# MLP products of a hybrid decoder layer: the first walks its moving operand and PSUM backwards, and the weights of both lie at other distances

## The reference

```python
h2 = rms_norm(x, pre_mlp_norm_w[layer])
a = jax.nn.relu(jnp.einsum("bsd,df->bsf", h2, w_ff1[layer]))
m_out = jnp.einsum("bsf,fd->bsd", a * a, w_ff2[layer])
x = x + rms_norm(m_out, post_mlp_norm_w[layer])
```

## Time and profile before

| | us |
|---|---|
| median of 2 runs | 2103.55 |
| lowest and highest | 2103.19, 2103.91 |
| the profiled execution | 2102.39 |
| its span, first to last instruction | 2100.2 |
| PE busy | 2070.8 |
| DVE busy | 1440.5 |
| ACT busy | 914.0 |
| POOL busy | 413.6 |

### The profile page before, as it was taken

One profiled execution on the slowest core, in us unless ns is written; L12 is line 12 of the kernel. 1 busy time (PEld: TensorE's weight loads), 2 busy tenths in 40 slices (PEclk: granted clock), 3 DMA queues, 4 the chain that ended last, 5 costly groups with the idle time before them and its releaser, 6 DMA issues. The chain is left out here.

```text
span 2100.2 us, 26863 instructions
## 1 busy us (share of the span) xinstructions
PE 2070.8 (99%) x10031; PEld 1736.0 (83%) x10031; DVE 1440.5 (69%) x1993; ACT 914.0 (44%) x1557; POOL 413.6 (20%) x252
## 2 busy tenths in 40 slices
PE   9999999999999999899999999999999999999998
PEld 9897878879788888688888788888888888888887
DVE  6897999889467777876667866666654536624285
ACT  6632434343444445745545644554431313313163
POOL 0000000000002312333332322332253034400012
PEclk9999999999999999999999999999999999999999
DMA  5121212113556875854455655445766455443376
GB/s 203 32 86 53 63 41 86 46 48 110 181 182 199 256 234 162 270 182 150 135 157 186 230 166 165 138 139 176 263 229 240 169 200 193 169 168 132 140 252 219
DMA packets 254143, 338.54 MB, mean 161 GB/s; under 512 B 11584, under 2 KB 195648, under 8 KB 240192
## 3 DMA queue, kind: packets, MB, share of 16 engines
q1 hardware_dynamic: 221376, 315.80, 45.1%
q10 hardware_dynamic: 32384, 20.98, 3.2%
q0 software_dynamic: 256, 0.07, 0.0%
HBM read 225.58 MB, written 111.21 MB: 160 GB/s over the span
## 5 line engine op out<-in xcount | busy, mean ns | idle before, releaser
L1953 PE MATMUL psum<-x_hi,w_hi_P 128*128 128x512 f32 x896 | 350.9, 392 | 10.7 <-DVE x_lo L1897 6.5
L1953 PE MATMUL psum<-x_lo,w_hi_P 128*128 128x512 f32 x896 | 349.8, 390 | 0.0
L2171 PE MATMUL psum<-w_hi,hid_hi 128*128 128x512 f32 x896 | 348.8, 389 | 0.9 <-DVE hid_lo L2049 0.9
L1953 PE MATMUL psum<-x_hi,w_lo_P 128*128 128x512 f32 x896 | 349.7, 390 | 0.0
L2171 PE MATMUL psum<-w_hi,hid_lo 128*128 128x512 f32 x896 | 348.6, 389 | 0.0
L2171 PE MATMUL psum<-w_lo,hid_hi 128*128 128x512 f32 x896 | 348.5, 389 | 0.0
L2049 DVE TENSOR_TENSOR hid_lo<-hid_raw,hid_hi 128x1024 fp32r<-128x1024 f32 x112 | 174.0, 1590 | 209.0 <-ACT hid_hi L2044 209.0
L2044 ACT ACTIVATE hid_hi<-hid_raw 128x1024 fp32r<-128x1024 f32 x112 | 113.0, 1051 | 342.5 <-DMA hid_raw<-scratch_hid 342.5
L1866 POOL TENSOR_TENSOR w_raw<-w_raw 128x512 f32<-128x512 f32 x128 | 181.2, 1440 | 409.3 <-DVE w_lo_P L1879 389.6
L1879 DVE TENSOR_TENSOR w_lo_P<-w_raw,w_hi_P 128x512 fp32r<-128x512 f32 x224 | 183.8, 833 | 106.5 <-ACT w_hi_P L1875 103.5
L1875 ACT ACTIVATE w_hi_P<-w_raw 128x512 fp32r<-128x512 f32 x224 | 136.8, 627 | 254.4 <-PE psum L1953 252.0
(11 more groups left out here) (284 smaller groups left out, 3814.7 us busy)
## 6 DMA issues: line engine op xcount, KB each, us to landing
scratch_hid<-stage SPq DMA_DIRECT2D x224, 256.0 KB, 3.7
hid_raw<-scratch_hid SPq DMA_DIRECT2D x56, 1024.0 KB, 4.9
w_raw<-in_w SPq DMA_DIRECT2D x52, 1024.0 KB, 5.0
w_grain<-in_w SPq DMA_DIRECT2D x48, 512.0 KB, 5.1
x_raw<-scratch_h2s SPq DMA_DIRECT2D x14, 1024.0 KB, 8.1
w_raw<-in_w_in SPq DMA_DIRECT2D x22, 512.0 KB, 3.6
scratch_h2s<-h2s SPq DMA_DIRECT2D x8, 1280.0 KB, 9.2
scratch_qk<-qout ACTq DMA_DIRECT2D x16, 512.0 KB, 3.4
```

Of the source, the lines that this page charges most:

```text
L1953: mm = nc.tensor.matmul(psum[:, bank_1(op, g), :], l, r, start=kt == 0 and i == 0, stop=kt == 3 and i == 2)
L2171: mm = nc.tensor.matmul(psum[:, bank, :], l, r, start=f == 0 and k == 0, stop=f == NFP - 1 and k == 2)
```

## The change

In the first product (`product`), the moving operand and the columns of PSUM are both indexed with `::-1`: the last token is read and written first, and each result lands at the address at which it landed before. The weight tiles move to other addresses, 128 bytes down and up again by 32 bytes after each third tile, so that there are five distances: w1_hi lies at -128, -96 and -64, w1_lo at -64, -32 and 0 bytes.

In the second product the slots of hid move: slot 0 by 256 bytes and another 16, slot 1 by 8, slot 2 by 0, and hid_lo and hid_raw of each slot by 32 more. The helper `hid_slot` allocates a tile with up to four floats more and leaves the first ones out. `acc` moves by 64 bytes, to make room.

```diff
-    w1_hi = {op: at(f"w1_hi_{op}", 69 + 2 * i, (4, P), F32R) for i, op in enumerate(OPS)}
-    w1_lo = {op: at(f"w1_lo_{op}", 83 + 2 * i, (4, P), F32R) for i, op in enumerate(OPS)}
+    w1_hi = {op: at(f"w1_hi_{op}", 68.875 + 2 * i + i // 3 / 32, (4, P), F32R) for i, op in enumerate(OPS)}
+    w1_lo = {op: at(f"w1_lo_{op}", 82.875 + 2 * i + (7 + i) // 3 / 32, (4, P), F32R) for i, op in enumerate(OPS)}
...
-    hid_at = [121, 48, 105]
-    hid_hi = [at(f"hid_hi{i}", kb, (NFP, P), F32R) for i, kb in enumerate(hid_at)]
-    hid_lo = [at(f"hid_lo{i}", kb + 8, (NFP, P), F32R) for i, kb in enumerate(hid_at)]
-    hid_raw = [at(f"hid_raw{i}", kb + 8, (NFP, P)) for i, kb in enumerate(hid_at)]
-    acc = [at(f"acc{t}", 64 + 4 * t if t < 10 else 97.5 + 4 * t, (D,)) for t in range(S // P)]
+    hid_at = [121 + 1 / 4, 48, 105]
+    hid_skip = [4, 2, 0]
+
+    def hid_slot(name, i, kb, dt=F32):
+        a = at(f"{name}{i}", kb, (NFP * P + hid_skip[i],), dt)
+        return a[:, hid_skip[i]:].rearrange("p (f t) -> p f t", f=NFP)
+
+    hid_hi = [hid_slot("hid_hi", i, kb, F32R) for i, kb in enumerate(hid_at)]
+    hid_lo = [hid_slot("hid_lo", i, kb + 8 + 1 / 32, F32R) for i, kb in enumerate(hid_at)]
+    hid_raw = [hid_slot("hid_raw", i, kb + 8 + 1 / 32) for i, kb in enumerate(hid_at)]
+    acc = [at(f"acc{t}", 64 + 1 / 16 + 4 * t if t < 10 else 97.5 + 4 * t, (D,)) for t in range(S // P)]
...
-                mm = nc.tensor.matmul(psum[:, bank_1(op, g), :], l, r, start=kt == 0 and i == 0, stop=kt == 3 and i == 2)
+                mm = nc.tensor.matmul(psum[:, bank_1(op, g), ::-1], l, r[:, ::-1], start=kt == 0 and i == 0, stop=kt == 3 and i == 2)
```

## The result

The changed kernel takes 2137.07 us (two runs, 2133.79 and 2140.36), before 2103.55 us: the ratio is 1.0155, interval 1.0138 to 1.0172, 33.5 us more. The forecast was 2090 us with a range to 2127 us: the sign was wrong, and the time lies 10 us above the range.

A forecast was written before the change was run, and what follows sets the result against it. The prediction took TensorE's matmul pace in the MLP as the bound. From the profiled 2102.4 us it took 13.4 us for the distances and nothing for direction, giving 2089.0, stated as 2090 us after allowing for the runs' median; range 2052 to 2127 us.

The forecast's parts named there:

- Bound and size of the pool: Both MLP products: only the pace of single matmuls is left to gain, 13.3 ns over 5,376 matmuls, 72 us.
- the other engines' cover: Second product, hid slots: some 10.5 us of transfer, ACT and DVE work fits in 21.8 us, so PE doesn't wait.
- I take no cost for the direction itself: First product: walking the moving operand and PSUM backwards costs nothing, the run being still contiguous.
- a walk at half the rate: Rival, first product: the backward walk is slow, 573 us more, 2676 us, a tenth of it 57 us; chance 0.07.
- Nearest rows: line 472, 10.8 ns in place of 13.3: Both products: new distances cost what line 472 (264 columns) pays over streaming; 5,376 x (13.3 - 10.8) = 13.4 us less.
- Both stages run through several distances, and a mean over distances is what that line is: Both products: reason for taking line 472's mean, 10.8 ns over streaming, not its best gap.
- the lock is lost: Rival, both products: changing distances never let the phase settle, 17.8 ns instead of 13.3, 24 us more, 2127 us; chance 0.22.
- The upper end: Whole kernel: top of the range to hold eight in ten, 2127 us.
- The edit on acc, hid_raw and the transfers at nothing: Second product: moving acc, and hid_raw with hid_lo, touches DVE, ACT and the transfers at no cost.
- unevenly, with a pattern that repeats: Starts of both products' matmuls: uneven gaps, in a pattern repeating with the group of hi, lo and slot.
- about 224 ns: Both products: expected spacing of matmul starts in the changed kernel's timeline, against 227 if distances don't matter.

The follow-up runs named there:

- the scan: Probe computing nothing of the reference: runs of 36 forward matmuls, 512 columns, distances 0 to 508 bytes in steps of 4; mean 232.0 ns a matmul.

## Why the prediction was wrong, point by point

- *Bound and size of the pool*: right. Nearly all of the difference (35.4 of 38.0 us between the two profiled executions) is in the two products, in the gaps between the starts of 5,376 matmuls, and the other engines' cover held.
- *"I take no cost for the direction itself"*: wrong, the second step that failed, from "the run is still contiguous" to "nothing changes". The backward walk of the moving operand costs 6.7 ns a matmul at distance 0 (213.3 + 20.0 in place of 213.3 + 13.3), 17.4 us measured. On top of the new distances it cost 2.1 ns more, so by itself it doesn't explain the sign. The rival had only a walk at half the rate in it; a cost between nothing and half the rate had no case of its own.
- *"Nearest rows: line 472, 10.8 ns in place of 13.3"*: wrong in sign, and the step that decided: this term of the sum stood at 13.4 us less and measured 30.8 us more (13.7 and 17.1 us, the distances of the two products alone, both operands forwards). The comparison itself was at fault: 13.3 ns is the cost of 256 and 512 columns at distance 0, and 264 columns cost 11.4 ns there. Its 264 columns were named as an objection, but only inside a rival. Measured for 512 columns, 18.6 ns for the first product's distances alone (231.9 - 213.3) and 19.3 ns for the second product's (232.6 - 213.3).
- *"Both stages run through several distances, and a mean over distances is what that line is"*: the idea of a mean over distances was sound for 512 columns, where it is 18.7 ns. I had the row for this as well: the nine unsettled gaps of the earlier trace rows at 231.1 ns, 17.8 over streaming, close to the 232.0 ns of the scan. It stood as the rival "the lock is lost" with 0.22 and 2127 us, and its size is near what the second product did. Its reason isn't: the phase does settle there, into other patterns that repeat (slot 0 with gaps of 231, 236 and 233 ns over and over), so the nearness of 17.8 to 19.3 ns is in part luck. The 512-column row should have weighed more than the 264-column one.
- *The upper end*: 2127 us was this rival's price with 17.8 ns. With 20.7 ns for the first product and 19.3 for the second the sum is 2,688 x (7.4 + 6.0) = 36 us, 2139 us. A rival's price from nine gaps was a mean, and the range ended on it, with nothing for the direction on top.
- *The edit on acc, hid_raw and the transfers at nothing*: right.
- *The trace, "unevenly, with a pattern that repeats"*: right for the second product, wrong for most of the first, where five of seven products ran at an even 233.3; the third and the fourth stood out in each g, by product and not by hi and lo alone. The pace, "about 224 ns", was wrong in both.

## What to carry to other kernels

When TensorE is busy throughout, read its pace from the starts and compare it with the columns' streaming time; the rest is a property of where both operands lie, and here it was worth up to 5% of a matmul's pace (226.7 to 237.8 ns). Price an edit of addresses only from rows with the same number of columns, and prefer a placement whose rhythm comes back after a disturbance (here distance 0, both operands forwards) to one that is as fast in one profile: the second kind can be 15 us slower in the next execution of the same program. Treat a mere turn of the order of reading as an edit with a cost of its own, and measure it alone.

## What the runs showed of the hardware

A float32r matmul of 512 columns with a weight load settled at 213.3 + 13.3 ns at best, and at no less in any of 512 placements tried; many stood at 20.0 ns over, and with several distances in turn single gaps went from 224 to 241 ns (the first product's distances alone). Part of the extra time may not come from the two reads at all: plain float32, which goes through at half the pace, had 2.9 ns over its streaming time. The Trainium skill (TensorE: Matmul & The Clock Gate, Part 2) says that the two SBUF read ports of TensorE are independent and that loading the next weights takes no read bandwidth from the running matmul. These runs differ: moving the weights by 8 or 32 bytes, all else equal, changes the matmul's pace by 4 to 7 ns (230.7 and 233.3 in place of 226.7). So the matmul's pace isn't independent of where the next weights are read; that the two reads meet somewhere is the likely reason, argued and not shown, and where (which memory line or bank) I did not settle; that it repeats after 256 bytes of distance, and depends on the moving operand's start with a period of 32 bytes, is measured, and a model of it is not.
